# Pairing narrow key tiles: tiles of 400 and 16, and of 272 and 144 query columns, share one unit of the FoX attention loop

## The reference, cut to what matters

```
log_f = jax.nn.log_sigmoid(ff + b_forget)
c_key = jnp.cumsum(log_f, axis=1)
logits = q @ k.T * ATTN_SCALE + (c_query - c_key)
logits = jnp.where(pos_query >= pos_key, logits, NEG_INF)
y_fox = softmax(logits) @ v * silu(z_fox)
m = sigmoid(gate_swa) * (y_swa @ w_up_swa) + sigmoid(gate_fox) * (y_fox @ w_up_fox)
h = h + rmsnorm(m @ w_out)
```

## Time and profile before

| | |
|---|---|
| median of 3 runs | 812.93 us (811.78 to 816.03) |
| the profiled execution, its own time | 811.67 us |
| its span | 809.9 us |
| PE busy in the span | 789.2 us (97%) |
| DVE / ACT / POOL busy | 481.1 / 315.4 / 340.7 us |

### The profile page before, as it was taken

The page is one execution under the profiler, slowest core; times in us unless marked ns, Lnnn a source line. Parts: engine busy times, 40 slices in busy tenths (PEclk is TensorE's granted clock), DMA queues, the critical chain, the costliest instruction groups (busy, mean ns, idle before and its releaser), DMA issues.

```text
span 809.9 us, 11838 instructions
## 1 busy us (share of the span) xinstructions
PE 789.2 (97%) x4058; PEld 624.0 (77%) x4058; DVE 481.1 (59%) x1006; ACT 315.4 (39%) x650; POOL 340.7 (42%) x287
## 2 busy tenths in 40 slices
PE   6999999999999999999999999999998999999996
PEld 4998889888888888888888865655554788878885
DVE  6835258577787777645646366677777634441222
ACT  6534022343334333333334337666767122231111
POOL 1132300765445535444445325758766335512221
PEclk9999999999999999999999999999999999999999
DMA  9344114479955435344344598999800665352222
GB/s 279 107 142 112 51 41 132 135 188 246 215 141 152 111 91 152 99 122 117 99 129 121 140 280 217 232 230 232 192 1 14 224 179 157 104 207 79 104 78 79
DMA packets 127813, 116.02 MB, mean 143 GB/s; under 512 B 29693, under 2 KB 102221, under 8 KB 127754
## 3 DMA queue, kind: packets, MB, share of 16 engines
q1 hardware_dynamic: 126456, 111.53, 51.8%
q10 hardware_dynamic: 1298, 3.74, 1.2%
HBM read 81.99 MB, written 34.96 MB: 144 GB/s over the span
## 4 chain that ended last, share of the span: by engine, by line
PE 88%; issue 4%; POOL 3%; DVE 3%; ACT 2%; DVEq 0%; ACTq 0%; POOLq 0%
PE PS L1986 21%; PE PS L1987 21%; PE PS L1988 21%; PE PS L2270 4%; PE PS L2272 4%; PE PS L2271 4%; PE PS L2192 3%; PE PS L2131 2%; POOL acc L1307 2%; PE PS L2172 1%; PE PS L2207 1%; PE PS L2173 1%; PE PS L2223 1%; PE PS L2018 1%; ACT p_fox L1480 1%
## 5 line engine op out<-in xcount | busy, mean ns | idle before, releaser
L1234 POOL TENSOR_TENSOR ops<-s_sum,ops 128x512 fp32r<-128x512 f32 x64 | 91.3, 1436 | 96.7 <-ACT ops L1336 96.7
L1234 POOL TENSOR_TENSOR ops<-raw,ops 128x512 fp32r<-128x512 f32 x48 | 67.9, 1416 | 118.8 <-ACT ops L1336 118.4
L1986 PE MATMUL PS<-t_hi,ops 128*128 128x512 f32 x256 | 100.1, 391 | 0.0
L1988 PE MATMUL PS<-t_hi,ops 128*128 128x512 f32 x256 | 99.9, 390 | 0.0
L1987 PE MATMUL PS<-t_lo,ops 128*128 128x512 f32 x256 | 99.9, 390 | 0.0
L1307 POOL TENSOR_TENSOR acc<-acc,p_fox 128x400 f32<-128x400 f32 (+5 forms) x76 | 61.4, 830 | 6.9 <-ACT p_fox L1480 5.8
L1480 ACT ACTIVATE p_fox<-PS,neg_c_col 128x512 f32<-128x512 f32 (+5 forms) x112 | 54.3, 536 | 13.0 <-PE PS L2178 8.5
L1804 DVE TENSOR_TENSOR z_tmp<-u,PS 128x512 f32<-128x512 f32 x48 | 32.9, 686 | 42.7 <-PE PS L1988 23.5
L1336 ACT ACTIVATE ops<-s_sum 128x512 fp32r<-128x512 f32 x64 | 39.4, 623 | 47.9 <-DVE s_sum L1588 42.8
L1988 PEld LDWEIGHTS PS<-t_hi,ops 128*128 128x128 f32 x256 | 48.1, 188 | 10.3
L1457 ACT ACTIVATE stage_b<-z_tmp,half_bg 128x512 f32<-128x512 f32 x32 | 23.2, 725 | 82.9 <-DVE z_tmp L1804 82.9
(11 more groups left out here) (237 smaller groups left out, 2040.9 us busy)
## 6 DMA issues: line engine op xcount, KB each, us to landing
raw<-in_w_in_dram SPq DMA_DIRECT2D x34, 512.0 KB, 5.3
g_dram<-stage_b SPq DMA_DIRECT2D x32, 256.0 KB, 2.0
tanh_g<-g_dram SPq DMA_DIRECT2D x16, 512.0 KB, 4.0
x_all<-in_x_dram SPq DMA_DIRECT2D x8, 512.0 KB, 7.3
raw<-in_w_in_dram SPq DMA_DIRECT2D x16, 256.0 KB, 4.7
q_dram<-stage_b SPq DMA_DIRECT2D x16, 256.0 KB, 2.8
q_swa_dram<-stage_b SPq DMA_DIRECT2D x16, 256.0 KB, 2.9
z_dram<-stage_b SPq DMA_DIRECT2D x16, 256.0 KB, 2.0
```

The costliest lines, as they stand in the source:

```text
L1234: nc.gpsimd.tensor_tensor(ops[:, i % OPS, 1], op_source(p, name), ops[:, i % OPS, 0].bitcast(F32), ALU.subtract).then_inc(op_ready, 1)
L1986: pe.matmul(dst, hi_w, hi, start=first, stop=False)
L1988: return pe.matmul(dst, lo_w, hi, start=False, stop=last)
```

## The change

Narrow tiles are put together in one unit: in half 0 tiles 1 and 4 (400 + 16 = 416 columns) and 2 and 3 (272 + 144 = 416), in half 1 tiles 5 and 8, and 6 and 7. The two share a score bank, a slot of `p_fox` and one step of values; each matmul, exponential and addition of before is still an instruction of its own. A pair has 10 units and the stage 40. The mask of a tile now directly follows that tile's scores, for each head. Tile 4 of half 0 computes 16 keys instead of 128 (the others were all masked). SWA items are spread one to each unit, units 2 to 33. The turns of loads, reciprocals, splits and up-projection pieces are rewritten for the new unit numbers.

```diff
+UNITS = (((0,), (1, 4), (2, 3)), ((0,), (1,), (2,), (3,), (4,), (5, 8), (6, 7)))
-REC_UNITS = ((4, 5, 6, 7, 8), (2, 3, 4, 5, 5))
-SECOND_LOADS = ((2, "load_queries", 0), (3, "load_keys", 0), (4, "load_values", 0), (8, "load_z", 0),
-                (9, "load_keys", 1), (10, "load_queries", 1), (11, "load_values", 1), (12, "load_z", 1))
+REC_UNITS = ((4, 5, 6, 7, 7), (2, 3, 3, 4, 4))
+SECOND_LOADS = ((2, "load_queries", 0), (2, "load_keys", 0), (3, "load_values", 0), (6, "load_z", 0),
+                (7, "load_keys", 1), (8, "load_queries", 1), (9, "load_values", 1), (9, "load_z", 1))
-NEXT_LOADS = ((1, "load_queries", None), (3, "load_keys", None), (5, "load_values", None), (6, "load_z", None))
+NEXT_LOADS = ((1, "load_queries", None), (2, "load_keys", None), (3, "load_values", None), (4, "load_z", None))
...
-    keys = min(P, LENGTH - P * i)
+    keys = min(P, r0 + w + N_META - P * i)
...
+def unit_tiles(q, tiles):
+
+    out, at = [], 0
+    for i in tiles:
+        r0, w, keys, masked, shift = key_tile(q, i)
+        out.append((i, at, r0, w, keys, masked, shift))
+        at += w
+    assert at <= BANK
+    return out
...
-    units = [(j, q, i) for j in range(PAIRS) for q in range(2) for i in range(4 * q + 5)]
+    units = [(j, q, tiles) for j in range(PAIRS) for q in range(2) for tiles in UNITS[q]]
     per = len(units) // PAIRS
-    spread = len(units) - 8 - FIRST_SLOT
+    spread = ITEMS
...
-                        pe.matmul(dst, KA[n][:, h, kk], QA[n][:, h, tok], start=True, stop=False)
-                        ins = pe.matmul(dst, KB[n][:, h, kk], QB[n][:, h, tok], start=False, stop=not masked)
-                        if not masked:
-                            ins.then_inc(tile_done, 1)
-                    if masked:
-                        for h in range(2):
-                            pe.matmul(PS[0:keys, S_BANKS[(2 * u + h) % S_RING], 0:masked], causal[:, 0:keys],
-                                      ident_b[:, shift:shift + masked], start=False, stop=True).then_inc(tile_done, 1)
+                        for i, at_, r0, w, keys, masked, shift in st["tiles"]:
+                            tok, kk = slice(r0, r0 + w), slice(P * i, P * i + keys)
+                            bank = PS[0:keys, S_BANKS[x % S_RING], :]
+                            dst = bank[:, at_:at_ + w]
+                            pe.matmul(dst, KA[n][:, h, kk], QA[n][:, h, tok], start=True, stop=False)
+                            ins = pe.matmul(dst, KB[n][:, h, kk], QB[n][:, h, tok], start=False, stop=not masked)
+                            if masked:
+                                ins = pe.matmul(bank[:, at_:at_ + masked], causal[:, 0:keys],
+                                                ident_b[:, shift:shift + masked], start=False, stop=True)
+                        ins.then_inc(tile_done, 1)
```

More of the change, by code:

```diff
@@ L279, in attention_steps @@
     closing = []
-    for u, (j, q, i) in enumerate(units):
-        first, last = i == 0, i == 4 * q + 4
+    for u, (j, q, tiles) in enumerate(units):
+        last = tiles == UNITS[q][-1]
         x = u % per
-        steps.append(dict(kind="tile", j=j, q=q, i=i, u=u, first=first, last=last))
+        steps.append(dict(kind="tile", j=j, q=q, i=tiles[0], u=u, tiles=unit_tiles(q, tiles)))
         if j + 1 < PAIRS:
@@ L297, in attention_steps @@
         if u:
-            pj, pq, pi = units[u - 1]
-            steps.append(dict(kind="values", j=pj, q=pq, i=pi, u=u - 1, first=pi == 0, last=pi == 4 * pq + 4))
+            pj, pq, before = units[u - 1]
+            steps.append(dict(kind="values", j=pj, q=pq, i=before[0], u=u - 1, tiles=unit_tiles(pq, before),
+                              last=before == UNITS[pq][-1]))
         if slot:
@@ L325, in attention_steps @@
             closing = merged
-        if split_ups and not slot and (j >= 2):
+        if j == 2 and x in UP_TURNS:
             d, half = split_ups.pop(0)
@@ L332, in attention_steps @@
                     steps.append(dict(kind="split_y", s=part, c0=c0, c1=c1))
-            if x == 13:
+            if x == per - 1:
                 steps.append(dict(kind="split_y", s=2 * PAIRS - 1, c0=0, c1=1))
-    j, q, i = units[-1]
-    steps.append(dict(kind="values", j=j, q=q, i=i, u=len(units) - 1, first=False, last=True))
+    j, q, tiles = units[-1]
+    steps.append(dict(kind="values", j=j, q=q, i=tiles[0], u=len(units) - 1, tiles=unit_tiles(q, tiles), last=True))
     for _, extra in closing:
@@ L834, in q_column @@
             return q_scale[:, j:j + 1] if kind == "qs" else q_scale[:, PAIRS:PAIRS + 1]
-        unit_of = {x: u for u, x in enumerate(units)}
+        last_unit = {(j, q): u for u, (j, q, tiles) in enumerate(units)}
         Q0, Q1 = slice(0, HEAD), slice(HEAD, P)
@@ L1297, in _ @@
                             continue
[L1298 to L1299 removed]
                         pool.wait_ge(fox_exp, n + 1)
[L1301 to L1307, removed]
+                        for k, (i, at_, r0, w, keys, masked, shift) in enumerate(st["tiles"]):
+                            c0 = r0 - BANK * q
+                            dst = acc[0:keys, f % 2, h, c0:c0 + w]
+                            tile = p_fox[0:keys, n % PT_RING, at_:at_ + w]
+                            if q == 0 and i == 0:
+                                nc.gpsimd.tensor_copy(dst, tile).then_inc(acc_done["pool"], 1)
+                                continue
+                            other = p_fox[:, (n - 2) % PT_RING, :] if (q, i) == (1, 1) else dst
+                            if (n, k) in acc_before:
+                                pool.wait_ge(*acc_before[n, k])
+                            nc.gpsimd.tensor_tensor(dst, other, tile, ALU.add).then_inc(acc_done["pool"], 1)
                 elif kind == "split_up":
@@ L2182, in _ @@
                     f = 2 * j + q
-                    r0, w, keys, masked, shift = key_tile(q, i)
-                    c0 = r0 - BANK * q
                     if u == 0:
                         pe.wait_ge(folded, n_fold)
-                    if st["first"] and f >= 2:
+                    if i == 0 and f >= 2:
                         pe.wait_ge(fox_y, f - 1)
@@ L2191, in _ @@
                         pe.wait_ge(fox_exp, x + 1)
-                        ins = pe.matmul(PS[h * HEAD:(h + 1) * HEAD, Y_BANKS[f % 2], c0:c0 + w],
-                                        VF[j % 2][0:keys, i, h * HEAD:(h + 1) * HEAD],
-                                        p_fox[0:keys, x % PT_RING, 0:w], start=st["first"], stop=st["last"])
+                    for k, (i, at_, r0, w, keys, masked, shift) in enumerate(st["tiles"]):
+                        c0 = r0 - BANK * q
+                        for h in range(2):
+                            ins = pe.matmul(PS[h * HEAD:(h + 1) * HEAD, Y_BANKS[f % 2], c0:c0 + w],
+                                            VF[j % 2][0:keys, i, h * HEAD:(h + 1) * HEAD],
+                                            p_fox[0:keys, (2 * u + h) % PT_RING, at_:at_ + w], start=i == 0,
+                                            stop=st["last"] and k == len(st["tiles"]) - 1)
                     ins.then_inc(fox_valued, 1)
```

52 lines of the change are left out of this document (25 added, 27 removed).

## The result

The changed kernel takes 820.7 us (median of 6 executions, 819.36 to 822.37) where the kernel before takes 813.2 (6 executions, 811.40 to 816.95): a ratio of 1.0094, 95% interval 1.0068 to 1.012. It is slower by 7.5 us. The prediction said 813.8, within 808.8 to 818.5. The profiled execution of after took 819.36 us with a span of 817.7.

What follows compares the result with a forecast made beforehand. It took PE, busy 97% of the span, as the bound, with scores 8 and 16 fixed by query loads in a full queue. 3.1 + 0.0 - 2.2 = +0.9 us gave 812.6 profiled, 813.8 at the median, range 808.8 to 818.5.

Steps and rivals of the forecast that it cites:

- Up to score 8: 0: Stage start to score 8: work PE saves is waited for at score 8, whose query load lands unchanged; 0 us.
- +3.1 us behind the anchor: Score 8 to score 16: score 16's start is fixed by its query load, so PE work moves behind it; +3.1 us.
- The three terms of PE's work: After score 16: eight merges -1.6 us, masks no longer adjacent +2.0, tile 4 with 16 keys -0.4; together 0.0.
- Waits: -2.2 us: After score 16: merged units give ACT more time and release head 0 earlier, cutting PE's 3.75 us idle; -2.2 us.
- Rival B: Ends of halves: crowded reciprocals and fin make DVE the bound, +5.9 us instead of -2.2, 821.9 us; chance 0.13.

Runs made afterwards that it cites:

- b2: The kernel before with only the mask of head 0 placed between the scores of head 0 and head 1; 812.3 us, ratio 0.9995.
- e1: The changed kernel with the reciprocals and fin of half 1 one unit earlier; 821.2 us, ratio 1.0107.
- s1: The changed kernel with every SWA item one unit later, starting at unit 3 instead of 2; 817.1 us, ratio 1.0054.
- s5: The changed kernel with SWA items one unit later and the values of pairs 2 and 3 loaded at turn 5 instead of 3; 814.2 us, ratio 1.0017.
- s6: s5 with the reciprocals of half 1 one step forward and fin alone in unit 4; 813.0 us, ratio 1.0005.
- h1_only: The changed kernel with tiles merged in half 1 only, 12 units to a pair and turns set for 12; 819.7 us, ratio 1.0077.
- b1: The kernel before with only fin of half 1 one unit later, right before the next pair's first half 1 values; 817.5 us, ratio 1.0064.

## Why the prediction was wrong

The size was wrong by 6.9 us (820.7 for 813.8) and outside of the range. Step by step:

- *"Up to score 8: 0"*: nearly so. Score 8 started 1.57 us late, at 513.12 instead of 511.55, with the load in place; this execution's stage itself began 1.40 us later, ahead of anything that was changed, and by score 16 all but 0.41 us of that was gone. The work saved turned into waiting, as said (2.58 us idle for 0.99), but at score 4, not at score 8.
- *"+3.1 us behind the anchor"*: right in kind. Score 16 started at 547.20 (546.8 predicted). PE was held by its load, though by 0.50 us and not the forecast 2 to 4: the wait for fin at 532.10, 2.13 us, had already used the slack. PE's busy time behind it grew by 2.19 us (predicted 3.1 and 0.0).
- *The three terms of PE's work*: their sum of 0.0 was near enough (-0.9 us, 2.19 less 3.1, if the moved work is taken as forecast). The masks were a little mis-sized: 0.07 us each was forecast and PE's busy time in b2 gives 0.054, so 28 of them 1.5 us instead of 2.0; and there 0.79 of 1.08 us came back as shorter waits. A merged pair of tiles of 272 and 144 columns saves little on the side of the scores; PE's timeline of after:

```profile
482.03 0.39 PE L2189 MATMUL PS<-QA,KA 128*128 128x272 f32 x1
...
483.41 0.34 PE L2163 MATMUL PS<-kk_s,QAs 128*128 128x208 f32 x1
...
484.02 1.11 PE L2208 MATMUL PS<-p_fox,VF 128*64 128x400 f32 x8
```

  From 482.03 to 483.41 are 1.38 us for what took 0.83 (480.92 to 481.75) and 0.61 us (482.57 to 483.18) in two units before: 0.06 saved. The load of 16 columns took 107 ns in after, by the group of weight loads:

```profile
L2189 PEld LDWEIGHTS PS<-QA,KA 128*16 128x16 f32 x16 | 1.7, 107 | 0.0
```

  This is near the 94 ns of the earlier trace rows. By the rule of the Trainium skill ("TensorE: Matmul & The Clock Gate", LDWEIGHTS) it would be 13 ns, an estimate. The trace does not agree with the rule here either, and it decided nothing.
- ***"Waits: -2.2 us"* is the step that failed.** Idle time behind score 16 rose by 4.54 us. Between -2.2 and +4.54 lie 6.7 us, nearly all of the 6.8 by which the profiled execution missed its forecast (819.36 for 812.6). The prediction looked for waits that a merge would shorten (short units waiting for their own exponential) and took the dependences at the ends of halves as they were. It never counted how many units were left between fin and the values that need its bank. These had been one; they became none, and two waits of 1.75 and 3.71 us stand there behind score 16. It also put the two longest waits of before down to "DVE and POOL", where its own rows have ACT (0.89) and "issue" (1.08); after has 0.80 for the latter.
- *Rival B* came nearest, in time (821.9) and in engine: DVE at the ends of halves. It had 0.13. Its sentence "Against: values are made one unit behind the exponentials, so PE has a unit's work in hand" was the error: the values of half 1 are exactly what waits, for the bank and not for the exponentials. Its mechanism was only half right: the burst of reciprocals alone did not hold PE, the bank did, at three places in the stage (two behind score 16, 1.75 + 3.71 = 5.46 us).
- *Why e1 did not repair it*: in e1 removing the fin waits changed only which of DVE's readers is late (14.52 us idle for 14.22). The loss is one of order: of items and loads, and of fin with them. Later items alone bring the ratio from 1.0094 to 1.0054 (s1), the values behind the queries to 1.0017 (s5), each clear of noise. The last step, the earlier reciprocals (s6, 1.0005), is not. With all of it the loss is gone, but nothing is won either, though over the three windows PE was busy 141.23 us for 143.60: what merging saves of PE's own work is at most 2.4 us, or 0.3%, and no run shows it in the time.

What stays open: what the small waits of h1_only have in common. That kernel has no wait for fin at all and is 0.8% slower, so the wait for fin is where the changed kernel lost time, but not the only way in which merging loses it.

## What to carry to other kernels

Where a loop gets fewer and larger steps, list for each wait across steps (a bank freed, a sum finished) how many steps lie between writer and reader before and after; a turn number that is scaled down can round the slack to nothing. In an in-order queue moving one late instruction forward makes another late; check which chain stands behind it before moving it. Place the loads and side work anew before judging a merge: here the same merge is 0.9% slower or even, by order alone, and it had at most 2.4 us of PE's own work to give.

## What the runs showed of the hardware

A wait can cost more than its length. Behind the wait of 2.18 us of b1 above, and those of 1.72 and 1.81 us in s5, PE's granted clock was at its lower level for 3.4 us; behind none of the waits of 2.13, 1.75 and 3.71 us in the profile of after was it. The window of s5 behind its wait of 1.72 us at 514.94:

```profile
515.00:518.40 3.40, 3.40 (x10) 1.43 (x12) 1.03 (x6) 1.01 (x4) 1.94 (x3) 0.53 1.07 235
```

The engine had worked without a gap since 514.94 and was still at 0.53. The Trainium skill ("TensorE: Matmul & The Clock Gate", Part 1) names the same two levels, 1.2 and 2.4 GHz. The windows shown, 0.51, 0.53 and 1.00, fit with it. Part of the spread of one kernel goes with the clock: b1 took 815.08 to 815.88 us in three executions (mean granted clock 0.995 to 0.997) and 820.55 to 821.21 in four with 0.989 to 0.991, with two between (816.98 and 817.45 us at 0.993 and 0.995); s5 took 811.83 to 812.85 us in five (0.996 to 0.999), 815.52 to 818.02 in the three with 0.994, and 814.09 to 815.32 in the other four, at 0.996 to 0.998. The profiled execution of after had none of these stretches before its last 6 us (clock 0.998) and was its fastest; its other five had 0.991 to 0.995 and took up to 3.0 us longer. This does not make the clock a part of the 7.5 us: the profiled execution of before had no such stretch ahead of its last 2 us either, and between the two lie 7.7 us (819.36 less 811.67).
